# Inverse roots of three recurrent heads: Newton steps on VectorE in place of ScalarE's root

## The reference, cut to what matters

```
h = num / maximum(abs(den), exp(-m))[..., None]        # per token and head, 128 values
h_ml = rmsnorm(h, ml_head_norm)                        # mean of squares over the 128 values
h_ml = h_ml * sigmoid(o_ml)
y = x * rsqrt(mean(x * x) + EPS) * g                   # what rmsnorm does
```

## Time and profile before

| What | us |
|---|---|
| Median of 3 runs | 1514.16 |
| The runs | 1514.08, 1517.75, 1514.16 |
| The profiled execution's own time | 1512.39 |
| Its span, first to last instruction | 1510.6 |
| PE busy | 1490.2 (99%) |
| DVE busy | 1128.3 (75%) |
| ACT busy | 751.5 (50%) |
| POOL busy | 627.2 (42%) |

### The profile page before, as it was taken

One profiled execution on the slowest core, in us unless ns is written; L12 is line 12 of the kernel. 1 busy time (PEld: TensorE's weight loads), 2 busy tenths in 40 slices (PEclk: granted clock), 3 DMA queues, 4 the chain that ended last, 5 costly groups with the idle time before them and its releaser, 6 DMA issues.

```text
span 1510.6 us, 20173 instructions
## 1 busy us (share of the span) xinstructions
PE 1490.2 (99%) x6978; PEld 1230.5 (81%) x6978; DVE 1128.3 (75%) x1872; ACT 751.5 (50%) x1255; POOL 627.2 (42%) x280
## 2 busy tenths in 40 slices
PE   9999999999999999999999999999999999999998
PEld 7888888878888887888888888786778888888887
DVE  5689999897875445776776768789755887777776
ACT  6553333454562345754544345464964745444434
POOL 3455444332334432144444445451544344444451
PEclk9999999999999999999999999999999999999999
DMA  5332333255543323323333123232653433333451
GB/s 212 98 126 98 98 95 95 89 158 156 158 156 98 98 83 112 102 94 98 112 98 107 54 84 98 84 98 88 181 151 106 144 114 92 109 121 114 142 136 56
DMA packets 77026, 170.40 MB, mean 113 GB/s; under 512 B 22660, under 2 KB 39172, under 8 KB 76680
## 3 DMA queue, kind: packets, MB, share of 16 engines
q1 hardware_dynamic: 75920, 165.64, 35.3%
q10 hardware_dynamic: 1016, 3.61, 0.7%
HBM read 154.54 MB, written 14.69 MB: 112 GB/s over the span
## 4 chain that ended last, share of the span: by engine, by line
PE 86%; DVE 4%; ACT 4%; issue 3%; POOL 1%; DMA 1%; SPq 0%; DVEq 0%; ACTq 0%; POOLq 0%
PE bank L795 86%; POOL w_lo L655 1%; DMA w_raw<-in_stream 1%; ACT w_hi L1604 1%; DVE x_sq L2359 0%; ACT l_probs L2129 0%; DVE bias L2441 0%; POOL res L764 0%; ACT l_probs L2135 0%; ACT dn_first L1898 0%; DVE qk_ml L2999 0%; DMA dn_raw<-in_stream 0%; PE bank L1214 0%; DVE res_tok L3420 0%; PE bank L905 0%
## 5 line engine op out<-in xcount | busy, mean ns | idle before, releaser
L655 POOL TENSOR_TENSOR w_lo<-w_raw,w_hi 128x1024 fp32r<-128x1024 f32 x191 | 472.5, 2484 | 519.2 <-ACT w_hi L1604 511.4
L795 PE MATMUL bank<-a_hi,w_hi 128*128 128x512 f32 (+1 forms) x1120 | 444.6, 397 | 1.8 <-DVE a_lo L3283 1.6
L795 PE MATMUL bank<-a_hi,w_lo 128*128 128x512 f32 (+1 forms) x1120 | 431.4, 385 | 0.0
L795 PE MATMUL bank<-a_lo,w_hi 128*128 128x512 f32 (+1 forms) x1120 | 431.2, 385 | 0.0
L1604 ACT CAST w_hi<-w_raw 128x1024 fp32r<-128x1024 f32 x199 | 204.6, 1046 | 174.2 <-DMA w_raw<-in_stream 174.1
L795 PEld LDWEIGHTS bank<-a_hi,w_hi 128*128 128x128 f32 x1120 | 210.5, 188 | 48.6 <-issue 3.9
L795 PEld LDWEIGHTS bank<-a_lo,w_hi 128*128 128x128 f32 x1120 | 210.5, 188 | 45.3 <-issue 3.4
L795 PEld LDWEIGHTS bank<-a_hi,w_lo 128*128 128x128 f32 x1120 | 210.4, 188 | 42.5
L667 POOL TENSOR_TENSOR dn_rest<-dn_raw,dn_second 128x1024 fp32r<-128x1024 f32 x39 | 93.7, 2433 | 248.3 <-DVE dn_rest L2734 248.3
L795 PE MATMUL bank<-dn_rest,f_hi 128*128 128x512 f32 x364 | 141.6, 389 | 0.0
L1898 ACT CAST dn_first<-dn_raw 128x1024 fp32r<-128x1024 f32 x54 | 55.6, 1049 | 157.8 <-DVE dn_raw L2715 157.8
(11 more groups left out here) (428 smaller groups left out, 2763.0 us busy)
## 6 DMA issues: line engine op xcount, KB each, us to landing
w_raw<-in_stream SPq DMA_DIRECT2D x199, 512.0 KB, 3.5
dn_raw<-in_stream SPq DMA_DIRECT2D x56, 512.0 KB, 3.5
p_parts<-d_parts SPq DMA_DIRECT2D x8, 640.0 KB, 3.9
d_turned<-p_parts SPq DMA_DIRECT2D x32, 160.0 KB, 3.3
l_turned<-p_parts SPq DMA_DIRECT2D x32, 160.0 KB, 3.0
p_parts<-l_parts SPq DMA_DIRECT2D x8, 384.0 KB, 3.4
res<-in_xT ACTq DMA_DIRECT2D x1, 2048.0 KB, 7.8
p_parts<-l_parts SPq DMA_DIRECT2D x8, 256.0 KB, 2.4
```

The source lines that it names most:

```text
L655: nc.gpsimd.tensor_tensor(w_lo[:, j, :], w_raw[:, j, :], w_hi[:, j, :].bitcast(F32), ALU.subtract).then_inc(w_lo_done, 1)
L795: return nc.tensor.matmul(o, l, r, start=start, stop=stop)
```

## The change

For heads 0, 1 and 2 ACT's square root at st 8 and DVE's reciprocal at st 9 go. In their place DVE computes the inverse root at st 8 in `ml_rest`: one operation on the bits of the number (a multiplication by -0.5 and an addition of a constant), and three Newton steps of three operations each, all of 128x4, each `chained` but the last. Head 3 keeps the root and the reciprocal. `ml_rest` now goes through the heads from the last to the first, so that head h+1's `negm_diag` (st 1) stands ahead of head h's inverse root (st 8) in the same step n. ACT's squares of head h now wait for head h-1's inverse root.

```diff
+ROOT_SEED = float(0x5F3759DF)
+ROOT_STEPS = 3
...
                 if st == 7:
                     act.wait_ge(sems["ml_out"], 4 * (h + 1))
+                    if h >= 1:
+                        act.wait_ge(sems["ml_inv"], h)
...
-                if st == 8:
+                if st == 8 and h == ML_HEADS - 1:
                     act.wait_ge(sems["ml_var"], h + 1)
                     A.activation(mcol[:, 3, :], mcol[:, 2, :], ACT.Sqrt).then_inc(sems["ml_root"], 1)
...
+            def inverse_root(h):
+                x, part, y = mcol[:, 2, :], mcol[:, 0, :], mcol[:, 3, :]
+                dve.wait_ge(sems["ml_var"], h + 1)
+                chained(V.tensor_scalar(y.bitcast(I32), x.bitcast(I32), -0.5, ROOT_SEED, ALU.mult, ALU.add))
+                for i in range(ROOT_STEPS):
+                    chained(V.scalar_tensor_tensor(out=part, in0=y, scalar=-0.5, in1=y, op0=ALU.mult, op1=ALU.mult))
+                    chained(V.tensor_tensor(part, part, x, ALU.mult))
+                    m = V.scalar_tensor_tensor(out=y, in0=part, scalar=1.5, in1=y, op0=ALU.add, op1=ALU.mult)
+                    if i < ROOT_STEPS - 1:
+                        chained(m)
+                    else:
+                        m.then_inc(sems["ml_inv"], 1)
...
+                if st == 8 and h < ML_HEADS - 1:
+                    inverse_root(h)
                 if st == 9:
-                    dve.wait_ge(sems["ml_root"], h + 1)
-                    V.reciprocal(mcol[:, 3, :], mcol[:, 3, :]).then_inc(sems["ml_inv"], 1)
+                    if h == ML_HEADS - 1:
+                        dve.wait_ge(sems["ml_root"], 1)
+                        V.reciprocal(mcol[:, 3, :], mcol[:, 3, :]).then_inc(sems["ml_inv"], 1)
                     dve.wait_ge(sems["ml_inv"], h + 1)
...
             def ml_rest(n):
-                for h in range(ML_HEADS):
+                for h in reversed(range(ML_HEADS)):
                     ml_step(h, n - ML_START - ML_EVERY * h)
```

## The result

The changed kernel takes 1525.05 us (median, 1524.31 to 1526.41), the kernel before 1514.08 (1512.47 to 1517.75). The forecast was 1528.8. One execution of `changed_again`, 1665.67 us at a mean granted clock of 0.848, is in a slow state and is left out of every comparison. The profiled execution is 1525.28 with a span of 1523.4, against 1512.39 and 1510.6 before: 12.8 us more in the span.

The account below looks back on a forecast made before the run. PE, busy for 99% of the span, was taken as the bound. Terms 1.3 + 0.7 + 1.1 + 5.3 + 3.2 = +11.6 us, plus 3 for PE's clock, +14.6, on the median 1514.16 gave 1528.8 us; range 1518 to 1535.

Parts of the forecast that it names:

- Head 0: First term: DVE's longer root makes `sT` of head 1, `hml` and PE's value matmuls late, +1.3 us.
- Head 1: Root delays `sT` of head 2, +0.7 us; its operations wait for three POOL operations, +5.3 us.
- Head 2: Root less DVE's idle time before `sT`, +1.1 us; its operations wait for two POOL operations, +3.2 us.
- The clock: PE's holes at heads 1 and 2 may drop its clock to 1.2 GHz; 0 to 5.5 us, taken as 3.
- The sum: Over the stage: head terms of +11.6 us plus 3 for PE's clock, together +14.6 us.
- The carried offset: Whole kernel: the shown median, 1514.16, lies 1.8 us above the profiled 1512.39; carried over to the forecast.
- the narrower 1526 to 1531: Whole kernel: the forecast case with a clock cost of 0 to 5.5 us, given a chance of 0.68.
- Rival 2: Beside POOL, tiny operations slip in without standstill: only +3.1 us, 1517.3, or about +6.5; chance 0.16.
- Rival 3: At head 1 POOL does not run dry, nine POOL operations: +7.6 us over the forecast, 1536.4; chance 0.09.
- Rival 1: In the stage ACT's chain is what counts: all four PE holes close, -3.6 us, 1510.6; chance 0.07.

Follow-up runs that it names:

- changed_again: The changed kernel run once more with no edit; ratio 1.0085 to the kernel before, compared executions 1524.57 to 1526.64 us.
- head0_alone: The changed kernel with the change for head 0 only, heads 1 and 2 keeping ACT's root; 1513.33 us against 1512.32 before, ratio 1.0004.
- one_in_psum: The changed kernel with the full root, but `y` in spare PSUM columns, so at most one input in SBUF; 1513.8 us against 1511.68 before, ratio 1.0014.
- reciprocals: The changed kernel with nine chained SBUF-to-SBUF reciprocals replacing the Newton operations, root not computed; one execution, 1515.58 us against a median of 1511.68 before.
- psum_one_step: `one_in_psum` with one Newton step instead of three and the root behind the next unit's reciprocal and mask; 1511.91 us against 1511.68 before, ratio 1.0002.
- pool_behind_roots: The changed kernel with POOL's two work lists waiting for the roots of heads 1 and 2 instead of diagonals; 1516.0 us against 1512.02 before, ratio 1.0029.
- pool_late_before: The kernel before with POOL's two work lists released by the reciprocals of heads 1 and 2 instead of diagonals; 1512.95 us against 1512.32, ratio 1.0005.

## Why the prediction was right

By its own steps, forecast beside measured.

- Head 0: 1.3 forecast, 0.74 measured (head0_alone repeats 0.73). This is the term that was mis-sized. The root took 1.85 us against 2.0, so 1.65 and not 1.8 without the reciprocal, and `sT` came at 1068.77, which with the lead of 1.28 is 1.4 late. The 0.23 us between were slack ahead of `sT`. In before it started that much behind the operation ahead of it (1068.40), just after ACT's `decay` had ended (1068.54); in the changed kernel it started with it. I had looked for such slack only at heads 1 and 2.
- Head 1: 0.7 + 5.3 = 6.0 forecast, 6.65 - 0.74 = 5.9 measured. The root ran from 1084.52 to 1091.67, 7.15 us against 7.3. `one_in_psum`, with nothing blocked, has 0.6 (1.28 - 0.70) for the 0.7. That the 1.41 us ahead of `sT` were a wait for ACT's `decay` the row doesn't say (it has "issue"), but ACT's `decay` ended at 1088.65, just ahead of `sT` at 1088.73, and in the changed kernel the wait was gone.
- Head 2: 1.1 + 3.2 = 4.3 forecast, 12.00 - 8.32 = 3.7 measured. The root took 5.1 us against 5.15; PE's hole was 3.84, not 4.4. A part of DVE's lateness is hidden there by the lateness that the clock had given PE by then, which I had left out. `reciprocals`, the only run with a chain of nine, none of the nine blocked and no fall at head 1, has 0.8 (2.37 - 1.58) in place of the 1.1; `one_in_psum`, with nothing blocked but a fall of 1.6 at head 1, has 0.02.
- The clock: 3 forecast, 1.67 + 1.88 = 3.55 measured. That both holes bring it down was held likely for one and open for the other. That the size came out is in good part luck: the 3 was a choice in the middle of 0 to 5.5, and the 5.5 took the lower level to last as long as the holes, 11 us. It lasted 2 x 6.8 us, of which 2.2 us lay in the first hole and none in the second; what it costs is half of the work that it covers, less what PE would have waited anyway.
- The sum: 14.6 forecast, 13.9 measured at the end of the stage and 14.06 at the last column. Less the lead, 12.8 in the span.
- The carried offset: I added 1.8 us for the distance of before's median from its profile. In the later comparisons before's median was 1511.7 to 1512.6, like its profile, so these 1.8 us belonged to the runs shown and not to the kernel. The changed kernel's median, 1525.05, lies 0.2 under its own profiled 1525.28. Of the 3.8 us between forecast and result, 1.8 are this, 1.3 the lead of the one profile, and the rest the terms and the 0.2. The range of 1518 to 1535 holds the result; the narrower 1526 to 1531, which the forecast itself had been given, misses it by 1 us.

The rivals. Rival 2 (no standstill) is refuted by the rows at head 1, and what its world would look like stands in `one_in_psum`: 2.1 us (1.0014) where it had 3.1. Rival 3 (nine blocked) was a matter of one rounding, as it said: moved one step, six are blocked and 4 us more are lost; its count of nine was too high. Rival 1 needs a root that costs DVE less than about 0.7 us. The 0.6 net of `psum_one_step` is such a one, and the gain is 0.96 us at its best place and not 3.6.

No version beats the kernel before. `psum_one_step` equals it, with two of three steps left out; the complete root without the standstill, `one_in_psum`, is 0.14% slower.

## What to carry to other kernels

Before work is moved to VectorE, look at what GpSimd does at that very place: a chain of N small operations of a kind that is blocked pays up to N whole GpSimd operations, not one, and here the count was how many GpSimd had ready. Keeping one operand in PSUM, or using an operation that isn't blocked, removed it; putting GpSimd off moved a part of it. An engine that is 96% busy in a stage need not be the one to relieve: the idle time of the engine that would be next (here DVE's 0.5 to 1.4 us) limited how much could be won.

## What the runs showed of the hardware that was not expected

- A tensor_scalar of 128x4 with one SBUF input is blocked like the two-input operations (2349 ns for 170), though the forecast spoke of two operands only; a reciprocal of the same size is not (178 ns), as its one row before had shown. Nor was a tensor_scalar that reads SBUF and writes PSUM: in `psum_one_step` the operation on the bits took 201 ns at 1083.72, beside POOL's operation of 1083.47 to 1085.85.
- TensorE's clock also fell behind small holes: behind 1.93 us (`head0_alone`), behind 1.19 and 0.48 (`pool_behind_roots`), behind 1.25 and 0.78 (`pool_late_before`). Each time it was at 1.2 GHz for 3.4 us, nearly all of them with work, and PE came out 1.6 us later. The kernel before has holes of 1.24 and 0.78 us at the same place and kept its clock in the one profile. Its other executions did not always: every profile with one such fall has a mean granted clock of 0.998, that of before has 0.999, and of the 67 executions of before timed beside the variants 22 show 0.998 or 0.997. Their median is 1513.3 us, that of the other 45, at 0.999 or 1.000, 1511.6. So the same kernel loses some clock in about a third of its executions, and the small falls in single profiles are not of the change alone. Where in the kernel these 22 lost it, and why one execution falls and another doesn't, stays open. `pool_late_before` shows 0.998 or 0.997 in 9 of 12; whether the put-off work makes a fall more frequent is not shown.
- A fall's cost differs between executions of one kernel, 1.67 and 1.13 us at head 1, with 6.8 us at the lower level both times; it goes by how much of PE's work lies in them, 4.6 and 3.5 us. With 1.88 and 1.65 us at head 2, the falls make 0.8 of the 1.1 us between the last columns of the changed kernel and `changed_again`.
